# Re-ordering three engines' hand-written programs in the RWKV block of a four-layer model plus two hybrid layers

## The reference, cut to what matters

```python
rkv = einsum('bsjd,jde->bsje', xm[:, :, :3], w_rkv)       # r, k, v
decay, a, g = ...                                          # low-rank products
if v_res is not None:                                      # only in layer 3 (n=1)
    v = v + (v_first - v) * sigmoid(v0 + (xv @ v1) @ v2)
for t in range(S):     # 16 heads, each with a 64x64 state
    sa = state @ kk_t
    state = state * w_t - outer(sa, kk_t * a_t) + outer(v_t, k_t)
    y_t = state @ r_t
y = group_norm(y) * ln_w + ln_b + sum(r * k * r_k) * v
out = (y * g) @ w_out
```

## Time and profile before

| | |
|---|---|
| time of the profiled execution | 1898.48 us |
| its span, first to last instruction | 1896.5 us (1.98 us lie outside) |
| three timed runs | 1898.48, 1899.74, 1897.82 us; median 1898.48 us |
| TensorE busy | 1810.1 us, 95% |
| VectorE busy | 1218.4 us, 64% |
| ScalarE busy | 1044.9 us, 55% |
| GpSimd busy | 68.1 us, 4% |
| mean granted TensorE clock | 0.978 |

### The profile page before, as it was taken

How to read it: one execution, slowest core, us unless ns; L and a number is a source line. 1 busy time by engine, 2 the same in 40 slices (tenths; PEclk the granted TensorE clock), 3 DMA queues, 4 the chain that set the end, 5 groups by cost and what they waited for, 6 DMA issues and landing times.

```text
span 1896.5 us, 41717 instructions
## 1 busy us (share of the span) xinstructions
PE 1810.1 (95%) x17879; PEld 1622.3 (86%) x17879; DVE 1218.4 (64%) x1783; ACT 1044.9 (55%) x1623; POOL 68.1 (4%) x58
## 2 busy tenths in 40 slices
PE   6999999999989999898999999999999999998998
PEld 5898798899979888797698888898798898887887
DVE  6853578865437675485768857754577756765764
ACT  5855465555436554364665545855465554564554
POOL 0001000000000000113000000001000000000000
PEclk8999999999999999899899999999999999999998
DMA  6330255557657656455475562420256564443441
GB/s 193 123 100 4 78 189 183 193 186 247 200 177 245 198 176 192 119 157 180 135 206 181 191 194 91 133 84 4 69 179 199 177 190 153 134 156 111 142 134 67
DMA packets 288526, 287.75 MB, mean 152 GB/s; under 512 B 15240, under 2 KB 286456, under 8 KB 288344
## 3 DMA queue, kind: packets, MB, share of 16 engines
q1 hardware_dynamic: 285048, 283.98, 47.3%
q10 hardware_dynamic: 3296, 1.11, 0.3%
HBM read 284.03 MB, written 1.05 MB: 150 GB/s over the span
## 4 chain that ended last, share of the span: by engine, by line
PE 90%; DVE 5%; ACT 2%; issue 1%; DMA 1%; POOL 0%; SPq 0%; DVEq 0%; ACTq 0%; POOLq 0%
PE ps L412 23%; PE ps L413 12%; PE ps L389 10%; PE ps L390 9%; PE ps L391 9%; PE ps L812 2%; PE ps L429 2%; PE ps L430 2%; PE ps L431 2%; PE ps L708 1%; PE ps L788 1%; PE ps L670 1%; PE ps L797 1%; PE ps L722 1%; PE ps L636 1%
## 5 line engine op out<-in xcount | busy, mean ns | idle before, releaser
L456 DVE TENSOR_TENSOR wl<-raw,wh 128x1024 fp32r<-128x1024 f32 x484 | 585.6, 1228 | 341.4 <-ACT wh L446 336.8
L446 ACT ACTIVATE wh<-raw 128x1024 fp32r<-128x1024 f32 x484 | 499.5, 1042 | 447.5 <-PE ps L413 191.3
L412 PE MATMUL ps<-HH,wh 128*128 128x512 f32 x1408 | 489.7, 391 | 0.0
L413 PE MATMUL ps<-HH,wl 128*128 128x256 f32 x1408 | 397.0, 282 | 0.0
L412 PEld LDWEIGHTS ps<-HH,wh 128*128 128x128 f32 x1408 | 264.3, 188 | 55.6 <-issue 0.4
L389 PE MATMUL ps<-HH,wh 128*128 128x256 f32 x928 | 271.1, 292 | 11.9 <-DVE HH L2552 6.2
L413 PEld LDWEIGHTS ps<-HH,wl 128*128 128x128 f32 x1408 | 266.1, 189 | 0.1
L390 PE MATMUL ps<-HH,wh 128*128 128x256 f32 x928 | 262.7, 283 | 0.0
L391 PE MATMUL ps<-HH,wl 128*128 128x256 f32 x928 | 262.3, 283 | 0.0
L389 PEld LDWEIGHTS ps<-HH,wh 128*128 128x128 f32 x928 | 178.5, 192 | 21.6 <-issue 4.9
L390 PEld LDWEIGHTS ps<-HH,wh 128*128 128x128 f32 x928 | 178.5, 192 | 1.3 <-issue 1.2
(11 more groups left out here) (323 smaller groups left out, 2962.8 us busy)
## 6 DMA issues: line engine op xcount, KB each, us to landing
raw<-in_ffn_w_gu_dram SPq DMA_DIRECT2D x88, 1024.0 KB, 5.1
raw<-in_ffn_w_down_dram SPq DMA_DIRECT2D x32, 1024.0 KB, 5.2
raw<-in_w_in_dram SPq DMA_DIRECT2D x32, 1024.0 KB, 5.7
raw<-in_rw_w_rkv_dram SPq DMA_DIRECT2D x24, 1024.0 KB, 5.6
B<-in_w_ada_dram SPq DMA_DIRECT2D x24, 1024.0 KB, 7.9
raw<-in_ds_w_in_dram SPq DMA_DIRECT2D x14, 1024.0 KB, 5.2
raw<-in_ffn_w_down_dram SPq DMA_DIRECT2D x16, 768.0 KB, 4.5
raw<-in_sb_w_qkv_dram SPq DMA_DIRECT2D x12, 1024.0 KB, 5.5
```

The costliest lines, as they stand in the source:

```text
L412: e.matmul(o[:, m, :], h_[:, k, c], x_, start=k0 + k == 0, stop=False, skip_group_check=True)
L413: i = e.matmul(o[:, m, 0:S], l_[:, k, c], x_[:, 0, :], start=False, stop=k0 + k == kt - 1, skip_group_check=True)
L446: e.activation(wh[:, u % UNITS, 0:kn * 256], raw[:, j % RAW, k0 * 256:(k0 + kn) * 256], ACT.Copy).then_inc(*up("hi"))
L456: e.tensor_tensor(wl[:, u % UNITS, 0:kn * 256], raw[:, j % RAW, k0 * 256:(k0 + kn) * 256], wh[:, u % UNITS, 0:kn * 256].bitcast(F32), ALU. ...
```

## The change

It re-orders instructions in `pe_rwkv`, `act_rwkv` and `dve_rwkv`. No instruction is added or removed, and no shape is changed.

- TensorE: the Gram products bp go ahead of unit 14; `value_rates` (now written in place) moves from behind level 2's second products to between units 14 and 15; pTM moves behind `second_products(32)`; behind it the order is pTM, br, V, kr, bTM, G, kTM, tp, term instead of V, br, bTM, G, kTM, kr, term, tp. `cur["bank"]` is no longer set at either place, only `cur["first"]`.
- ScalarE: the sigmoids of n=1 and the `eye` activation go ahead of the copy of receptance block 3 and of all levels; in each level one `hi` stands between the xs copies and the turn copies, where both `hi` stood behind the turn copies or ahead of the xs copies; the table load goes ahead of turn 16, the tt copies ahead of pTM, the tp copies ahead of term.
- VectorE: one `lo` more is done ahead of the levels; in each level `lo` and the small work (`key_decay`, `read_decay`, `own_term`) come ahead of `level` instead of behind it; `value_mix` of block g moves to the head of the next level.

```diff
--- before.py
+++ after.py
@@ -840,7 +840,14 @@
                     else:
                         quarters("low", m, j, Tw, X1, "dve")
 
-            def value_rates():
+            cur["first"] = 1
+            for j in range(2):
+                gram("pb", j, Pm, Bt_)
+            for j in range(2):
+                gram("bp", j, Bt_, Pm)
+            last_read = block_halves(0, 1, 3)
+            next(last_read)
+            if n:
                 e.wait_ge(*at("act", ("gv", n)))
                 e.wait_ge(s_v2, 16)
                 for g in range(4):
@@ -849,36 +856,27 @@
                         c = slice(g * 256 + m * P, g * 256 + m * P + P)
                         i = e.matmul(o[:, m * S:(m + 1) * S], v2_up[:, c], lor[32:64, :], start=True, stop=True, skip_group_check=True)
                     i.then_inc(*up("mm", ("v2", n, g)))
-
-            last_read = block_halves(0, 1, 3)
-            cur["first"], cur["bank"] = 1, bank_of["full", n, 0, 2]
-            for j in range(2):
-                gram("pb", j, Pm, Bt_)
             next(last_read)
-            for j in range(2):
-                gram("bp", j, Bt_, Pm)
-            for _ in last_read:
-                pass
             for g in range(4):
                 first_products(LEVELS[g])
                 values = block_halves(2, 0, g)
                 next(values)
                 second_products(LEVELS[g])
-                if n and g == 0:
-                    value_rates()
                 next(values)
             first_products(32)
             for j in range(2):
                 gram("kp", j, Kp, Pm)
+            second_products(32)
+            cur["first"] = 0
             for j in range(2):
                 pe_to_tm(e, ("pTM", n, j), Pm, j)
-            second_products(32)
-            cur["first"], cur["bank"] = 0, bank_of["tt", n, 32, 1, 1] + 1
+            for j in range(2):
+                gram("br", j, Bt_, R_)
             e.wait_ge(*at("dve" if n else "act", ("vmix", n, 3) if n else ("full", n, 2, 3)))
             for j in range(2):
                 pe_to_tm(e, ("V", n, j), v_, j)
             for j in range(2):
-                gram("br", j, Bt_, R_)
+                gram("kr", j, Kp, R_)
             for j in range(2):
                 pe_to_tm(e, ("bTM", n, j), Bt_, j)
             for j, par in groups:
@@ -889,12 +887,6 @@
                 product(o, j, par, Lk, lambda a, p_: V[half(a), j, hd(p_):hd(p_) + HD]).then_inc(*up("mm", ("G", n, j, par)))
             for j in range(2):
                 pe_to_tm(e, ("kTM", n, j), Kp, j)
-            for j in range(2):
-                gram("kr", j, Kp, R_)
-            for g in range(4):
-                o = bank(e, ("term", n, g), ("act", ("term", n, g)))
-                e.wait_ge(*at("dve", ("term", n, g // 2)))
-                e.matmul(o[:, :], C("bones"), term[:, 2 * g:2 * g + 2, :], start=True, stop=True, skip_group_check=True).then_inc(*up("mm", ("term", n, g)))
             for j in range(2):
                 os = [bank(e, ("tp", n, j, a), ("act", ("tp", n, j, a))) for a in range(2)]
                 e.wait_ge(*at("act", ("pTM", n, j, 1)))
@@ -908,6 +900,11 @@
                                          start=True, stop=True, skip_group_check=True)
                             if p_ == 7 and par == 1:
                                 i.then_inc(*up("mm", ("tp", n, j, a)))
+
+            for g in range(4):
+                o = bank(e, ("term", n, g), ("act", ("term", n, g)))
+                e.wait_ge(*at("dve", ("term", n, g // 2)))
+                e.matmul(o[:, :], C("bones"), term[:, 2 * g:2 * g + 2, :], start=True, stop=True, skip_group_check=True).then_inc(*up("mm", ("term", n, g)))
 
             jg, g2 = raw_piece(e)
 
@@ -1632,34 +1629,29 @@
 
             for j, par in groups:
                 copy_out(("bp", n, j, par), At[:, j, par, :])
-            hi(e, 1)
+            hi(e)
+            if n:
+                for g in range(4):
+                    sigmoids("v2", g, "rw_v0", vmix, 0)
+            e.wait_ge(*at("mm", ("gv", n)))
+            e.wait_ge(*at("dve", ("PB", n, 1)))
+            e.activation(BUF[0][:, :].rearrange("p (q t) -> p q t", t=HD), C("eye").unsqueeze(1).to_broadcast([P, 32, HD]),
+                         ACT.Copy).then_inc(*up("act", ("eye", n)))
+            evac(0, 3, R_)
             for g in range(4):
-                hi(e, 1)
-                if g == 0:
-                    evac(0, 3, R_)
-                elif n == 0:
-                    evac(2, g - 1, v_)
                 for j in range(2):
                     quarters_out("xs", LEVELS[g], j, X1)
+                hi(e, 1)
                 turned(LEVELS[g] // 2)
-                if g == 2:
-                    e.wait_ge(*at("mm", ("gv", n)))
-                    e.wait_ge(*at("dve", ("PB", n, 1)))
-                    e.activation(BUF[0][:, :].rearrange("p (q t) -> p q t", t=HD), C("eye").unsqueeze(1).to_broadcast([P, 32, HD]),
-                                 ACT.Copy).then_inc(*up("act", ("eye", n)))
                 hi(e, 1)
-                if n and g == 0:
-                    for q in range(4):
-                        sigmoids("v2", q, "rw_v0", vmix, 0)
-            hi(e, 1)
-            if n == 0:
-                evac(2, 3, v_)
+                if n == 0:
+                    evac(2, g, v_)
+            log_and_exp(e)
             turned(16)
-            log_and_exp(e)
+            for j in range(2):
+                quarters_out("tt", 32, j, Tn, -1.0)
             for j in range(2):
                 to_tm(("pTM", n, j), pTM[:, j, :])
-            for j in range(2):
-                quarters_out("tt", 32, j, Tn, -1.0)
             for j in range(2):
                 to_tm(("V", n, j), V[:, j, :])
             for j in range(2):
@@ -1668,13 +1660,13 @@
                 copy_out(("G", n, j, par), Lk[:, j, par, :])
             for j in range(2):
                 to_tm(("kTM", n, j), kTM[:, j, :])
-            for g in range(4):
-                e.wait_ge(*at("mm", ("term", n, g)))
-                e.activation(term[:, 2 * g:2 * g + 2, :], two(PS("term", n, g)[:, :]), ACT.Copy).then_inc(*up("act", ("term", n, g)))
             for j in range(2):
                 for a in range(2):
                     e.wait_ge(*at("mm", ("kTM", n, 1, 1)))
                     copy_out(("tp", n, j, a), TP[:, 2 * j + a, :])
+            for g in range(4):
+                e.wait_ge(*at("mm", ("term", n, g)))
+                e.activation(term[:, 2 * g:2 * g + 2, :], two(PS("term", n, g)[:, :]), ACT.Copy).then_inc(*up("act", ("term", n, g)))
 
             def negate_u(c):
                 j, a = c // 2, c % 2
@@ -2313,10 +2305,10 @@
                         e.copy_predicated(dst[:, j, :, a, :], low8(m), q8(PS(key, n, m, j, a)[:, :])).then_inc(*up("dve", (key, n, m, j, a)))
 
             lo(e)
-            lo(e, 1)
+            lo(e)
             for g in range(4):
-                lo(e, 1)
-                level("low", LEVELS[g], T)
+                if n and g:
+                    value_mix(g - 1)
                 lo(e, 1)
                 if g == 0:
                     key_decay(0)
@@ -2326,9 +2318,10 @@
                     read_decay(1)
                 if g > 1:
                     own_term(g - 2)
-                if n:
-                    value_mix(g)
-            lo(e, 1)
+                level("low", LEVELS[g], T)
+                lo(e, 1)
+            if n:
+                value_mix(3)
             e.wait_ge(*at("act", ("eye", n)))
             level("xs", 32, Xw)
             for j, par in groups:
```

## The result

The changed kernel takes 1950.23 us (median of 4 runs, 1948.94 to 1954.17) against 1899.11 us (1897.82 to 1900.73): 1.0272 times the time before, 95% interval 1.0254 to 1.029, so 51 us slower. 1936.6 us was forecast with a range up to 1946. The mechanism that carried most of the forecast is there to a tenth of a microsecond; a second one, which the forecast has no term for, is the largest part of what is missing; a clock term and a term for PSUM banks that were too small are the other parts.

The account below looks back on a forecast made before the run. TensorE, busy 1810.1 of 1896.5 us, was taken to bound the kernel, so its waits add in full. 1898.5 + 29.1 (n=0 9.7, n=1 19.4) + 9.0 for the clock = 1936.6 us; own range 1930 to 1942, all but the last case 1922 to 1946.

Parts of the forecast that it names:

- The `hi` in eight levels: Turn copies queue behind a `hi` awaiting a later unit; low waits 2.4 us a level, 14.4 us for six levels.
- T+9.25: Start of low, counted from T, when a level's xs products start; T+6.85 in the kernel before.
- Level 2 behind `eye` and the sigmoids: ScalarE's earlier work delays level 2's first xs copy and low: 3.3 us in n=0, 6.8 us in n=1.
- `value_mix` late: Levels 4, 8, 16 of n=1: `value_mix` behind `lo` frees bank 0 0.8 us late for the value unit; 2.4 us.
- VectorE's small work hidden: Small work ahead of `level` priced at nothing, as the second unit hides it; without that cover up to 2.8 us a level.
- The clock: Ten new waits of 2 us or more; six taken to cause a half-clock stretch of about 1.5 us each: 9.0 us.
- falls behind every wait: Rival: ten half-clock stretches at 1.5 us, 15 us in all, giving 1942.6 us; chance 0.12.
- the clock holds: Rival: the waits come but no clock falls, giving 1927.6 us; chance 0.18.
- the start of the levels costs nothing: Rival: bank waits, level 2's extras and `value_mix` (10.5 us) are hidden, giving about 1922 us; chance 0.06.
- The products behind the levels: Behind the levels: n=0 gains 1.6 us with tt ahead of pTM; in n=1 neither of the two waits exists.
- both go: -1.6 us: n=0: pTM's 1.23 wait for a copy and br's 0.34 wait for a mask were both to vanish.
- The banks: Without the reset pb waits for receptance block 2's copy, 0.8 us (n=0), 2.0 (n=1); pTM's second group 1.0 (n=1).

Follow-up runs that it names:

- b_hi: Kernel before with one `hi` of each level put between the xs copies and the turn copies on ScalarE; 1929.35 us, 1.0163.
- b_early: Kernel before with `value_rates` between units 14 and 15, sigmoids and `eye` ahead of receptance block 3's copy, levels' order left; 1903.57 us, 1.0026.
- b_dve: Kernel before with VectorE's order of the changed kernel alone; 1906.66 us, 1.0048.
- b_gram: Kernel before with the Gram products bp directly behind pb, ahead of unit 14, in both layers; 1901.89 us, 1.0016.
- b_gram192: Kernel before with only the first half of bp directly behind pb, the second half behind unit 14; 1899.28 us, 1.0002.
- a_hold: Changed kernel with the load of value block 2's weights held back until bp is done; 1936.26 us, 1.0197.
- b_tail: Kernel before with the changed order of products behind the levels on TensorE and ScalarE, bank counter still set by hand; 1897.48 us, 0.9991.
- b_banks: Kernel before without the two lines that set the bank counter; 1905.23 us, 1.0036.
- b_hold: Kernel before with bp directly behind pb and the load of value block 2's weights held until bp is done; 1899.67 us, 1.0003.
- a_banks: Changed kernel with the two lines back that set the bank counter; 1939.56 us, 1.0221.
- a_again: Changed kernel, unedited, run once more for a second profile; the profiled execution took 1948.81 us.

## Why the prediction was right, and where it failed

**The `hi` in eight levels: right.** 2.4 us a level was forecast with T+9.25 for low; the wait is 2.49 us and low starts at T+9.41 in level 4 of n=0. b_hi alone is 31 us of the 51, its clock included.

**Level 2 behind `eye` and the sigmoids: right, a little too large.** Forecast 0.9 and 4.4 us beyond the common wait, 5.3 in all; b_early measured 5.0 (2.8 to 7.0), with 2.12 us at the fourth turn group, where it had been put. In the changed kernel low of level 2 starts at T+10.02 and T+12.94, where 10.15 and 13.65 had been forecast.

**`value_mix` late: right.** 0.8 us in three levels was forecast. In level 4 of n=1 the unit starts 4.6 us behind xs (1285.77 to 1290.35) instead of 3.9, released by VectorE, and nearly the same in the next two.

**VectorE's small work hidden: right, with its condition.** Nothing in the changed kernel; 7.7 us where the levels are short (b_dve). The forecast had said up to 2.8 us a level; the largest was 1.6.

**The clock: mechanism right, size too small.** 9.0 us were forecast, as six falls of 1.5 us. From pb to level 32 the lower clock costs 13 us in b_hi and 15.3 in the changed kernel, where seven of the eight waits in the levels are followed by low products of 2.9 to 3.6 us instead of 2.2. That is the size that the rival "falls behind every wait" had (15 us), though a part of it stands behind stops that no rival has; the rivals in which the clock holds and in which the start of the levels costs nothing are out. The page of the Trainium skill that was cited, "TensorE: Matmul & The Clock Gate", would have had no fall behind such waits; the runs decide against it, since behind waits of 2.49 us the half clock came in both layers (for one, TensorE's low products behind the second wait of n=1 take 3.49 us instead of 2.2). That none of the new waits reaches the page's length did not fit the forecast's own working, by which TensorE would have idled 4.25 us ahead of the fourth turn group in level 2 of n=1 (T+3.65 to T+7.9); it holds for what was measured there, 2.12 us.

**The step that failed** is the first of the change's list, "the Gram products bp go ahead of unit 14". The forecast gives it no term and no reason for having none: it prices only waits for another engine, waits for a bank, and the clock, and bp has none of the waits. The runs showed a resource that has no semaphore. Between units, 128 short matmuls are followed by 24 long ones; behind pb, 256 short ones come in a row, and the instructions of the last 29 to 51 are not there in time. b_gram shows it alone (3.9 us, 0.9 to 5.1), b_gram192 that a unit between is enough, a_hold that a weight load makes it more than twice as long in n=0. In the changed kernel the two stops are 3.27 and 2.46 us of idle time, with half clock behind them; from pb to level 2 that part took 10.8 us more where 0.8 had been forecast, and taking bp back gives 7.5 us. The sign of it was in the rows before: the second wait of the earlier trace rows, 0.34 us, says "issue", and the prediction read it as a wait for a mask. It was such a stop. The changed kernel has none in br, but one of 0.76 us in kr.

a_hold stands, at 1936.26 us, where the forecast had put the whole (1936.6). I count that agreement as luck: a_hold still has a stop of 1.22 us in n=0, and in pb to level 32 it gives back only 8 to 9 of its 14 us.

**The products behind the levels: half right.** The wait of 1.23 us for a copy went, but "both go: -1.6 us" counted the 0.34 with it and overlooked that kp and tt now stand back to back. b_tail measured -1.1 us with an interval that takes in zero, and the changed kernel has 0.7 us more there in n=0.

**The banks: waits right, price too small.** 3.8 us forecast, waits of 3.3 found, 6.7 us measured alone and 10.7 in the changed kernel.

**Still open.** Why the banks cost twice their waits alone, and what a_hold gives back outside the stretch that it touches. The profiles of single executions differ by as much as these: b_banks' runs spread over 13 us, those of the changed kernel over 11. That time at half clock feeds on every added idle stretch, so that the same edit costs more in a kernel that has many, fits and is argued, not shown.

## What to carry to other kernels

When the order of instructions on an engine changes, look not only at what each one waits for but at how the engine's instructions reach it: a stream of short matmuls may have nothing in its way and still stop, and a few long instructions between two short runs give the supply time to catch up. A short "issue" wait in the profile before is the sign to look for. And on an in-order engine never put an instruction whose release comes from later in the chain (`hi`, for a unit behind the turns) ahead of copies that the chain is waiting for (the turn copies); the other way round it cost nothing.

## What the runs showed of the hardware

TensorE's instructions arrive in packets of 16 KB (2.33 MB in 142 packets on the queue of the page, for 35,758 matmuls and weight loads, so about 250 of them, or 126 pairs, a packet; that this queue is TensorE's is read from these counts). The stops lie at fixed places of the instruction stream, 126 or 127 matmuls apart where two follow one another, which is one packet. Short 64x64 matmuls with their loads use up a packet in about 2.1 us at full clock. A stop in bp lasted 1.1 to 1.3 us with the weight load held back (a_hold, b_hold), 2.0 to 3.3 us beside a load that was under way (the changed kernel, b_gram's n=0, a_banks), and 1.14 us in b_gram's n=1, where the load had only just begun. Behind the levels, with nothing but instruction packets on the DMA queues in a_again, the stops were 1.85 and 1.70 us. At a granted clock of 0.52 and then 0.91 the same 256 pairs take 5.66 us and do not stop (a_hold, n=1). Such stops have no releaser in the profile ("issue"); the kernel before has a few of them as well, of 0.3 to 1.1 us, inside its short products.
